# Rotary embedding read from the accumulators by the vector engine, in a hybrid attention layer on one core

## The reference

```
h = x @ w_in
(qa, ka, va, gate_a, qb, kb, vb, gate_b, mg_a, mg_b) = split(h)
qa, ka, qb, kb = apply_rope(each, positions)
o_a = banded_attention(qa, ka, va, window 128, sinks)     # 16 heads of 64, 2 kv heads
o_b = dilated attention in 3 patterns, 4 heads of 128 each, mixed by softmax of the log-sums
y_a = (o_a * silu(gate_a)) @ w_pa ;  y_b = (o_b * silu(gate_b)) @ w_pb
merged = sigmoid(mg_a + b0) * y_a + sigmoid(mg_b + b1) * y_b
out = layer_norm(alpha * x + merged @ w_out)
```

## Time and profile before

| | |
|---|---|
| Median of 3 runs | 1379.71 us (1379.18 to 1380.14) |
| The profiled execution, whole | 1380.62 us |
| Its span, first to last instruction | 1378.8 us |
| PE busy | 1359.5 us, 99% |
| DVE busy | 479.4 us, 35% |
| ACT busy | 574.7 us, 42% |
| POOL busy | 671.2 us, 49% |
| Mean granted clock of PE | 0.997 of full speed |

### The profile page before, as it was taken

The page is one execution under the profiler, slowest core; times in us unless marked ns, Lnnn a source line. Parts: engine busy times, 40 slices in busy tenths (PEclk is TensorE's granted clock), DMA queues, the critical chain, the costliest instruction groups (busy, mean ns, idle before and its releaser), DMA issues.

```text
span 1378.8 us, 19889 instructions
## 1 busy us (share of the span) xinstructions
PE 1359.5 (99%) x6488; PEld 1153.5 (84%) x6488; DVE 479.4 (35%) x846; ACT 574.7 (42%) x971; POOL 671.2 (49%) x512
## 2 busy tenths in 40 slices
PE   9999999999999999999999999999999999999996
PEld 7888888888988988898898888888888888888884
DVE  4866665662030223204111011010101202287688
ACT  5465464543471374356247222222222222445442
POOL 4633443455455556546454555464555636422214
PEclk9999999999999999999999999999999999999998
DMA  8442241445374355337444344653536446377674
GB/s 258 132 127 77 76 137 49 134 115 126 91 167 144 81 115 141 124 86 167 145 111 141 89 151 117 144 139 101 171 94 159 123 127 146 98 246 259 202 253 154
DMA packets 204990, 190.07 MB, mean 138 GB/s; under 512 B 16528, under 2 KB 178576, under 8 KB 204944
## 3 DMA queue, kind: packets, MB, share of 16 engines
q1 hardware_dynamic: 191344, 151.74, 37.8%
q0 software_dynamic: 13600, 37.75, 11.3%
HBM read 185.23 MB, written 41.94 MB: 165 GB/s over the span
## 4 chain that ended last, share of the span: by engine, by line
PE 68%; issue 16%; POOL 11%; DMA 2%; DVE 1%; ACT 1%; POOLq 0%; SPq 0%; ACTq 0%
PE acc L1517 61%; POOL w_lo L577 6%; POOL w_lo L576 5%; PE ps_scores L1517 2%; DMA raw<-w_in 1%; PE ps_out L1517 1%; PE ps_turn L1517 1%; PE ps_out L1607 1%; DMA raw<-w_out 0%; PE ps_turn L1579 0%; DVE z L1375 0%; PE ps_scores L1544 0%; DMA raw<-xT 0%; PE ps_scores L1541 0%; DVE x_lo L983 0%
## 5 line engine op out<-in xcount | busy, mean ns | idle before, releaser
L576 POOL TENSOR_TENSOR w_lo<-raw,w_hi 128x512 fp32r<-128x512 f32 x242 | 322.7, 1334 | 689.9 <-ACT w_hi L630 567.9
L1517 PE MATMUL acc<-x_hi,w_hi 128*128 128x512 f32 x1216 | 477.9, 393 | 0.0
L1517 PE MATMUL acc<-x_hi,w_lo 128*128 128x512 f32 x1216 | 474.2, 390 | 0.0
L1517 PE MATMUL acc<-x_lo,w_hi 128*128 128x512 f32 x1216 | 474.0, 390 | 0.0
L630 ACT ACTIVATE w_hi<-raw 128x1024 fp32r<-128x1024 f32 x224 | 234.2, 1056 | 338.8 <-PE acc L1517 330.0
L577 POOL TENSOR_TENSOR w_lo<-raw,w_hi 128x512 fp32r<-128x512 f32 x242 | 333.7, 1379 | 0.0
L1517 PEld LDWEIGHTS acc<-x_hi,w_lo 128*128 128x128 f32 x1216 | 228.2, 188 | 48.0
L1517 PEld LDWEIGHTS acc<-x_hi,w_hi 128*128 128x128 f32 x1216 | 228.5, 188 | 44.3 <-POOL w_lo L577 0.2
L1517 PEld LDWEIGHTS acc<-x_lo,w_hi 128*128 128x128 f32 x1216 | 228.5, 188 | 44.1
L1240 DVE TENSOR_TENSOR part_a<-acc,part_a 128x512 f32<-128x512 f32 x16 | 11.1, 691 | 321.7 <-PE acc L1517 321.5
L1517 PE MATMUL acc<-w_hi,x_lo 128*128 128x384 f32 x256 | 85.6, 334 | 0.0
(11 more groups left out here) (275 smaller groups left out, 1605.4 us busy)
## 6 DMA issues: line engine op xcount, KB each, us to landing
raw<-w_in SPq DMA_DIRECT2D x384, 128.0 KB, 2.3
q_left<-w_out POOLq DMA_DIRECT2D x12, 2048.0 KB, 13.6
raw<-w_in SPq DMA_DIRECT2D x256, 96.0 KB, 2.6
raw<-q_left SPq DMA_DIRECT2D x32, 512.0 KB, 4.7
raw<-w_in SPq DMA_DIRECT2D x64, 192.0 KB, 3.0
raw<-w_pa SPq DMA_DIRECT2D x64, 128.0 KB, 6.1
raw<-w_out SPq DMA_DIRECT2D x16, 512.0 KB, 4.4
raw<-xT SPq DMA_DIRECT2D x8, 512.0 KB, 5.0
```

What stands on the lines that cost most here:

```text
L576: nc.gpsimd.tensor_tensor(dst[:, left], raw[:, slot, left], hi[:, left].bitcast(F32), ALU.subtract)
L1517: ins = nc.tensor.matmul(into[:, 0:cols], s, m, start=start and k == 0, stop=stop and k == n - 1)
```

## The change

`swap_halves` and all its calls go, and so does the semaphore `swapped`. DVE now makes the exchange itself: the new `rope_sine` multiplies, out of the bank, the 32 or 64 rows of one half by the sines of the other half's place, so it is four instructions in branch A and two in branch B. It comes first, then `rope_cosine`, which frees the bank, then the addition, `rope_sum`. The pulled-ahead cosine of head 0 is gone. The last gate of a pass, unit 7's, is done after the rope of bank 0 and the split of q; in head 0, where it also stands at g = 26, after the three ropes at 23 to 25.

```diff
-            def swap_halves(dst, src, half, done):
...
-                    if last and bank < 2:
-                        act.wait_ge(full[bank], fills_a(bank, i) + 1)
-                        swap_halves((shifted, shifted_a)[bank][:], acc[bank][:], 32, ropes_a(i, 0))
...
             def rope_cosine(dst, src, src_full, src_free, filled, done, branch, cos):
 
                 to_order, from_order = orders(branch)
-                dve.wait_ge(src_full, filled)
-                dve.wait_ge(swapped, done + 1)
                 nc.vector.tensor_tensor(to_order(dst), from_order(src), from_order(cos[:]), ALU.mult).then_inc(src_free, 1)
 
-            def rope_sine(dst, swapped_src, src_free, filled, done, branch, sin):
+            def rope_sine(swapped_src, src, src_full, filled, done, step, sin):
+
+                dve.wait_ge(src_full, filled)
+                if not (isinstance(done, int) and done == 0):
+                    dve.wait_ge(rope_done, done)
+                for k in range(P // step):
+                    here, there = (slice(step * n, step * n + step) for n in (k, k ^ 1))
+                    last = nc.vector.tensor_tensor(swapped_src[here, :], src[there, :], sin[here, :], ALU.mult)
+                last.then_inc(rope_parts, 1)
+
+            def rope_sum(dst, swapped_src, src_free, filled, done, branch):
 
                 to_order, from_order = orders(branch)
-                nc.vector.tensor_tensor(swapped_src, swapped_src, sin[:], ALU.mult).then_inc(rope_parts, 1)
                 dve.wait_ge(rope_parts, done + 1)
                 dve.wait_ge(src_free, filled)
                 nc.vector.tensor_tensor(to_order(dst), to_order(dst), from_order(swapped_src), ALU.add).then_inc(rope_done, 1)
...
-                    elif stage == "values" and kind == "a":
+                    elif stage == "values" and kind == "a" and u < A_UNITS - 1:
                         gate_out(kind, u, a, i)
...
+                    if with_attention and ("values", A_UNITS - 1) in A_PLAN.get(g, ()):
+                        gate_out("a", A_UNITS - 1, unit_a(i - 1) + (A_UNITS - 1), i - 1)
                     if A_BLOCKS[g - 1][2:4] == (A_JOBS - 1, 1):
                         rope_q(i, 1)
...
-                        ahead = first and done_group == 0
-                        if not (ahead and tile == 2):
-                            rope_b_cosine(h, done_group, tile)
-                        if ahead and tile == 1:
-                            rope_b_cosine(h, 0, 2)
-                        rope_b_sine(h, first, done_group, tile)
+                        rope_b(h, first, done_group, tile)
+                    if first and ("values", A_UNITS - 1) in A_PLAN.get(g, ()):
+                        gate_out("a", A_UNITS - 1, unit_a(A_ITERS - 1) + (A_UNITS - 1), A_ITERS - 1)
```

More of the change, by code:

```diff
@@ L330, in build @@
         sink_step, sink_set = sem("sink_step"), sem("sink_set")
-        swapped, rope_parts, rope_done = sem("swapped"), sem("rope_parts"), sem("rope_done")
+        rope_parts, rope_done = sem("rope_parts"), sem("rope_done")
         v_out, v_turned, v_hi_ready, v_a_ready = sem("v_out"), sem("v_turned"), sem("v_hi_ready"), sem("v_a_ready")
@@ L770, in iter_a @@
                         nc.scalar.activation(by_block(vT_a[:]), by_residue(ps_out[:]), ACT.Copy).then_inc(v_out, 1)
-                        swap_halves(shifted[:], ps_scores[:, 0:SEQ], 32, 0)
                     if not with_attention and g == 13:
@@ L791, in iter_a @@
                         high(job_a(i), job + AHEAD)
-            def swap_first():
-                act.wait_ge(full[0], fills_b(0, 0) + 1)
-                swap_halves(shifted[:], acc[0][:], 64, ropes_b(0, 0))
             def iter_b(h, first):
@@ L800, in iter_b @@
                     if first:
-                        attend("a", A_PLAN, g, unit_a(A_ITERS - 1), A_ITERS - 1, swap_first if g == 21 else None)
+                        attend("a", A_PLAN, g, unit_a(A_ITERS - 1), A_ITERS - 1)
                     else:
                         attend("b", B_PLAN, g, unit_b(h - 1), h - 1)
[L804 to L811, removed]
                     if last and group == 1 and bank == 3:
@@ L1018, in rope @@
             def rope(dst, swapped_src, src, src_full, src_free, filled, done, branch, cos, sin):
+                rope_sine(swapped_src, src, src_full, filled, done, 32, sin)
                 rope_cosine(dst, src, src_full, src_free, filled, done, branch, cos)
-                rope_sine(dst, swapped_src, src_free, filled, done, branch, sin)
+                rope_sum(dst, swapped_src, src_free, filled, done, branch)
             def masked(dst, scores, mask, scale, least):
@@ L1200, in rope_q, with rope_b @@
                 rope(q_a[:, j, :], (shifted, shifted_a)[j][:], acc[j][:], full[j], free[j], fills_a(j, i) + 1, ropes_a(i, j), "a", cos_a, sin_a)
-            def rope_b_cosine(h, group, tile):
-                rope_cosine((q_b, k_b)[group][:, tile, :], acc[tile][:], full[tile], free[tile], fills_b(tile, h) + (group + 1),
-                            ropes_b(h, 3 * group + tile), "b" if tile else "a", cos_b)
-            def rope_b_sine(h, first, group, tile):
-                rope_sine((q_b, k_b)[group][:, tile, :], swap_place(first, group, tile), free[tile], fills_b(tile, h) + (group + 1),
-                          ropes_b(h, 3 * group + tile), "b" if tile else "a", sin_b)
+            def rope_b(h, first, group, tile):
+                filled, done, place = fills_b(tile, h) + (group + 1), ropes_b(h, 3 * group + tile), swap_place(first, group, tile)
+                rope_sine(place, acc[tile][:], full[tile], filled, done, 64, sin_b)
+                rope_cosine((q_b, k_b)[group][:, tile, :], acc[tile][:], full[tile], free[tile], filled, done, "b" if tile else "a", cos_b)
+                rope_sum((q_b, k_b)[group][:, tile, :], place, free[tile], filled, done, "b" if tile else "a")
             def iter_b(h, first):
```

2 lines of the change are left out of this document (1 added, 1 removed).

## The result

Changed kernel: median of 4 runs 1395.57 us (1394.29 to 1396.69). Before, on the same chip: 1379.45 (1378.85 to 1380.14, 4 runs). The ratio is 1.0116, 95% interval [1.0103, 1.0128]: slower by 16.1 us, where 11.3 were forecast, at the upper end of the range (0.07 above 1395.5). The profiled executions differ by the same (spans 1394.9 and 1378.8).

The account below looks back on a forecast made before the run. PE, busy 99%, bounds the kernel; DVE's order at pass boundaries decides when PE goes on. Four boundaries 7.9 us plus head 0 3.4 = 11.3, on a median of 1379.71: 1391.0 us, range 1385 to 1395.5.

Parts of the forecast that it names:

- The price of an exchanged product: DVE's products out of a bank: 0.69 us each, also for the cosine product behind them; 0.60 the low end.
- rival (a): Products follow each other by 0.60: boundaries and head 0 cost less, 7.4 us, 1387; chance 0.25 together with (d).
- (b): Not slower: products below 0.43 us each, DVE keeps up, 1378.3; chance 0.10, including DVE keeping up for another reason.
- The boundary before pass 3: Where a pass ends: q ready before PE needs it, PE waits 2.1 us for bank 1, net cost 2.4.
- (d): PE's wait for bank 1 is all, the chain over ACT catches up: 7.5 us, 1387; chance 0.25 with (a).
- The boundary before pass 1: First boundary, without a last gate: 4.2 - 1.6 - 1.9 = 0.7 us cost, bounds -0.7 and 2.4.
- Head 0: Ropes of banks 1 and 2: PE waits 1.05 and 2.3 us, together 3.4; 2.4 with an addition clear of POOL.
- rival (c): PE's clock falls to 1.2 GHz behind each of five new waits: 6.8 us more, 1398; chance 0.05.
- list of signs: New profile: 0.69 us products, no PE wait for q's split, new bank waits; wrong if granted clock below 1.0 at boundaries.
- What costs nothing: Heads 1 to 3 and group 1 of head 0: added products covered by DVE's idleness; ACT's copies worth nothing.
- wanted by nobody: Last gate, behind all three ropes of head 0: not needed before head 0's own gate, so it costs nothing.
- a high end: Range's top: 11.3 + 1.5 + 1.7 = 14.5 for additions under POOL and first boundary, and 1 for the heads: 1395.5.

Follow-up runs that it names:

- the second tile was moved: Changed kernel with ACT's second tile of q moved from in front of unit 0's exponentials to behind unit 0's copy of its probabilities: 1391.03 us, ratio 1.0083.
- both from copies and the late second tile: Kernel before with ACT's second tile of q late, gate moved, bank 0 of each pass and heads (except head 0's first three ropes) exchanged on DVE: 1376.93 us, 0.9976.
- kernel with filled waits: Changed kernel with idle PE transpositions of the identity before bank 1 of passes 1 to 3 and banks 1 and 2 of head 0: 1393.37 us, 1.0093.

## Why the prediction was right, and where it was off

**The price of an exchanged product** held. The changed kernel's products of 32 rows take 679 to 697 ns and four take 2.79, so 0.70 from start to start; predicted 0.69. The bound of 0.60, and rival (a) with it, falls; so does (b), which needed 0.43. The Trainium skill's rule (VectorE: DVE Perf Modes, Two Vector instructions with no wait between them) agrees with these starts.

**The boundary before pass 3** held link by link. On the time scale of before (7.64 less): q ready at 187.9 (188.2 predicted), bank 1 free at 193.5 (193.7), PE's wait 1.89 (2.1), the chain's end 2.2 late (2.4). The addition took 0.69, not 1.2: POOL was wholly out of the way. Of that 0.5, 0.2 went on the start (181.2, not 181.0), and 0.2 on the gaps inside each rope. That the chain over ACT, not PE's wait, sets the end is shown by the 0.51 behind the 1.89, and by its going when the second tile was moved. So (d) was wrong in its mechanism.

**The boundary before pass 1** is the step that failed: "I take 1.6, since the rope of k with its 2.1 us more of products runs into it", and then "The addition and the casts come clear of POOL, which gives 1.0 + 0.9". The second half happened (the addition 0.69, the casts 0.87). But q's rope began at 72.44, 1.7 later than the 70.76 of before, where the assumed 1.6 would have put it at 69.2. Part of this could be read beforehand. In the kernel before:

```profile
70.76 0.69 DVE L1008 TENSOR_TENSOR q_a<-acc,cos_a 128x512 f32<-128x512 f32 x1 [2.52 <-ACT shifted L737]
```

DVE's row of k ended at 68.24, so 2.1 more of products leave 0.4 of the start and not 1.6. The prediction had no row of this place. Then k's subtractions took 1.0 longer under the very POOL job that had left q's row: I had booked where the collision went from and not where it went to. The remainder is start-up: DVE came to k's rope 1.3 later (57.47 against 56.15), PE to this place 0.6, and kernels with the same program up to here scatter as much (DVE 55.89 to 57.47). The boundary cost 3.8 instead of 0.7: PE waits 2.20 for q, 1.45 for bank 1 and 0.52 for the remainder, against 0.73 in all before. The runs divide it: with k from copies 2.7, with bank 1 from copies 1.6, with both from copies and the late second tile 0.2. So bank 1's exchange is 2.1 and k's 1.1, and the gain of 3.5 that was set against them (1.6 and 1.9) came only in its second half.

**Head 0**: waits of 1.07 and 2.05 for 1.05 and 2.3, since bank 1's addition took 1.39 under POOL and not 1.67. PE lost 3.7 to 3.8 by them where its clock stood at 1.00, and 1.6 more by the clock.

**The clock**, rival (c) at 0.05, was not all or nothing: it fell behind two of the waits, 2.5 us at the same matmuls, 2 to 3 by the medians and ratios of the kernel with filled waits. A share of it belonged in the sum of the forecast. By the prediction's own list of signs two went against it: the clock below 1.0 at a boundary, and a wait for the split of q, 2.20 before pass 1.

**What costs nothing** held: heads 1 to 3 and group 1 of head 0 (0.1 us measured), and ACT's copies. The moved gate, "wanted by nobody", needed more care than it got: the prediction counted it as 2.0 in DVE's row and was right, but did not say that without it q would be 2.6 late, 1.9 of it by POOL's job coming to lie over the gate's split.

So the sign, the mechanism and the places were right, and the size of the first boundary was not. 4.8 us were missing. In the profiled executions: 3.1 at the first boundary, 2.5 of clock (0.9 before pass 2, 1.6 in head 0), 0.4 in head 0's waits and 0.6 of start-up; against them 0.4 less before pass 3 and head 0, and 1.4 in the rest. Of that 1.4, 1.3 are waits that the change does not touch (0.6 for 1.4 on a transpose's probabilities, 0.4 for 0.9 on the last weights). That the result stayed at the edge of the range owes something to this luck, and to a high end whose terms, 14.5 and 1, add up to 1395.2 and not to 1395.5. One more sum was off: the 11 us of new products in branch B are 24 times 0.69, 16.6. DVE's whole came out at 20 because the new products add 30 (some of the old ones had run longer under POOL) and the additions, clear of POOL, take 10 less.

## What to carry to other kernels

An engine that is 35% busy can be full for the 12 us that count. List its instructions between the transfer that starts them and the one PE waits for, and price an added instruction there at its full length; elsewhere it is free. When a part of a change takes work off one engine, look for the job of a third engine that was held back by it, and at what it will now lie over. Compare two traces at the same matmuls before you explain a stretch: part of the difference can be older than the change. And edits in one row of work do not add: try them one by one and together before either is judged.

## What the runs showed that was not expected

- The same edit, the moved gate, is 5.3 us slower with copies and 6 faster with exchanged products (1380.2, 1385.5; 1401.7, 1395.6).
- PE's granted clock fell behind waits of 2.13 and 2.05 us in one kernel, to 1.2 GHz for about 3 us, and stayed at 1.00 behind waits of 2.12 and 2.03 in another at the same places. In two others it fell before pass 1, behind waits for q of 1.96 and 2.18, and not in the changed kernel behind 2.20; with the gate back it fell behind the wait of 2.58 before pass 3, and not behind 2.58 and 2.59 at the other two boundaries. What decides it is open.
- Four subtractions of 64 rows on DVE take 3.82, 4.81 or 5.77 us, as more or less of POOL's jobs of the same time lies over them (1.1, 3.5 and 4.3 us of POOL's work).
